# The final norm inside the experts' stage: all rows first, the last three tiles' rows apart

## The chip, the cores and the metric

The kernel runs on one core of a Trainium2 chip. The metric is the device time of one execution in microseconds (us), the median of several. The core has five engines that run on their own and meet at semaphores: TensorE (PE) multiplies matrices, VectorE (DVE) and ScalarE (ACT) work on elements, GpSimd (POOL) issues the indirect DMAs, SyncE (SP) the plain ones. All DMAs run on the core's 16 DMA engines.

## The reference

One decoder layer over 2048 prompt rows and 64 sample rows of 1024 channels. Only its end matters here:

```python
h2 = modulate(rmsnorm(x, prm['norm2_g']), sh2, sc2)
x = x + g2[:, None, :] * hier_moe(h2, ...)      # top-1 of 4 groups, top-2 of its 4 experts
...
y_prompt = rmsnorm(xp, final_norm_g)
y_sample = rmsnorm(xs, final_norm_g)
```

`rmsnorm` divides a row by the root of its mean square plus 1e-6 and multiplies by a gain per channel. Every row goes through exactly two of the 16 experts; an expert is `silu(t @ w_gate) * (t @ w_up)`, times the gate, `@ w_down`.

## The kernel before

`front` and `middle` compute everything up to `h2`. They leave in DRAM `h2_d` (the normed rows), `acc_d` (2112 rows that hold x for the prompt and zeros for the samples, and 128 rows more for the empty places of tiles) and `x2s_d` (x of the samples). `routing` sorts the row numbers by expert into tiles of 128 places. With this input there are 43 tiles, numbered 0 to 42, and `last` is 42.

`experts` takes the tiles in turn. SyncE loads an expert's 3 MiB of weights two experts ahead, once the splits of the expert two before are done (`W.load`). GpSimd gathers a tile's rows from `h2_d` and, four tiles later in its order, scatters a finished tile's rows onto `acc_d` with an adding indirect DMA (`scatter`, line 2241). A scatter waits for the one before it to land, since two tiles can hold the same row, and only then frees its output buffer (`freed`). TensorE transposes the rows, multiplies by gate and up weights, transposes the hidden rows and multiplies by the down weights; each product is made of three, of high and low parts, which ScalarE and VectorE split off. VectorE's `out` (line 2363) multiplies the product by the gating row and leaves it in `o_sb`. ScalarE, VectorE and GpSimd run this in a loop of two tiles a round, with straight code for the last tile. Each engine goes through its own instructions strictly in the order in which they are written; nothing else orders the work.

When all 43 scatters have landed GpSimd raises `all_added`, and `final_norm` begins. SyncE reads `acc_d` in eight pairs of 128-row tiles (1 MiB each, 8 KiB a row) and the sample rows with `x2s_d` (lines 2497 to 2500). For each tile ScalarE squares and sums (2517), VectorE makes the mean (2533), ScalarE the root (2520), VectorE the reciprocal (2535) and the normed rows (2537). SyncE stores each finished pair (2507) and, at the end, waits for all stores.

## Time and profile before

| | us |
|---|---|
| median of 3 executions | 1243.48 (1240.98 to 1244.09) |
| the profiled execution, its own time | 1243.06 |
| its span, first to last instruction | 1241.1 |
| TensorE busy in the span | 1049.5 (85%) |
| VectorE, ScalarE, GpSimd busy | 755.6, 514.4, 258.4 |
| last product on TensorE ends | 1185.2 |
| last scatter lands | 1193.7 |
| last norm on VectorE ends | 1234.9 |

Times in the rows further down are in us from the span's start. A timeline row gives start, duration, engine, source line, operation, what it writes and reads, and in brackets the idle time before it and what ended it. A row of windows gives busy time and count of instructions of each engine in a stretch, then the granted clock of TensorE (1.00 is 2.4 GHz, 0.50 is 1.2 GHz), the mean busy share of the DMA engines and what they moved.

### The profile page before, as it was taken

To read this page: it belongs to the slowest core of one execution; us is meant where nothing else is said; L and a number is where in the kernel's file an instruction comes from. 1 tells how busy PE (TensorE), PEld (TensorE's weight loads), DVE (VectorE), ACT (ScalarE), POOL (GpSimd) and SP (SyncE) were. 2 spreads that over 40 slices of the span, in tenths; PEclk is the share of its full clock that TensorE was granted. 3 is DMA by queue.
4 is the path that set the end of the run, shared out by engine and by line. 5 is a ranking of instruction groups with operands and counts; after the bars stand their busy time and mean duration, and the time that the engine had idled before them with its cause. 6 is when DMAs were issued, how large, how long until landed. Compare 5 with 4: busy or idle time off the path is not lost. (4 is left out here: it accounts for less than half of the span.)

```text
span 1241.1 us, 18046 instructions
## 1 busy us (share of the span) xinstructions
PE 1049.5 (85%) x5428; PEld 798.2 (64%) x5429; DVE 755.6 (61%) x1234; ACT 514.4 (41%) x764; POOL 258.4 (21%) x319
## 2 busy tenths in 40 slices
PE   5599999997568999997999535999999999999910
PEld 3266676674446767786888424887778878778710
DVE  2746475750289983367887686555676555555336
ACT  2522333221152235444665313455655544445325
POOL 0025252534131000000000001233333332232210
PEclk9699999998779999998999857999999999999955
DMA  9814646474592549466766457698789878765479
GB/s 304 324 35 115 205 114 201 118 228 162 147 198 90 167 140 265 157 175 233 239 209 224 134 201 250 163 293 217 218 263 267 223 212 222 220 154 110 88 206 394
DMA packets 173443, 244.74 MB, mean 197 GB/s; under 512 B 70519, under 2 KB 130631, under 8 KB 170263
## 3 DMA queue, kind: packets, MB, share of 16 engines
q1 hardware_dynamic: 148617, 180.31, 45.6%
q0 software_dynamic: 12528, 45.62, 16.1%
q10 hardware_dynamic: 12246, 18.14, 4.2%
q8 instruction: 29, 0.48, 0.1%
q14 instruction: 23, 0.19, 0.0%
HBM read 167.79 MB, written 75.84 MB: 196 GB/s over the span
## 5 line engine op out<-in xcount | busy, mean ns | idle before, releaser
L120 PE MATMUL experts_psGU<-weights_we_hi,experts_x_hi 128*128 (+1 forms) x344 | 144.9, 421 | 8.2 <-DVE experts_x_lo L2344 6.5
L121 PE MATMUL experts_psGU<-weights_we_hi,experts_x_lo 128*128 (+1 forms) x344 | 137.6, 400 | 0.0
L122 PE MATMUL experts_psGU<-weights_we_lo,experts_x_hi 128*128 (+1 forms) x344 | 137.5, 400 | 0.0
L120 PE MATMUL front_psM<-front_hT_hi,front_w_hi 128*128 128x512 f32 x256 | 105.7, 413 | 0.0
L2241 POOL DMA_INDIRECT acc_d<-experts_o_sb,experts_to_col x43 | 72.7, 1690 | 150.3 <-issue 67.0
L121 PE MATMUL front_psM<-front_hT_hi,front_w_lo 128*128 128x512 f32 x256 | 100.4, 392 | 0.0
L122 PE MATMUL front_psM<-front_hT_lo,front_w_hi 128*128 128x512 f32 x256 | 100.1, 391 | 0.0
L120 PEld LDWEIGHTS experts_psGU<-weights_we_hi,experts_x_hi 128*128 128x128 f32 x344 | 65.7, 191 | 34.1 <-issue 19.3
L2344 DVE TENSOR_TENSOR experts_x_lo<-experts_psX,experts_x_hi 128x1024 fp32r<-128x1024 f32 x44 | 53.9, 1225 | 40.1 <-ACT experts_x_hi L2277 40.1
L2334 DVE TENSOR_TENSOR weights_we_lo<-weights_we_raw,weights_we_hi (+1 forms) x64 | 75.5, 1220 | 4.1 <-ACT weights_we_hi L2268 3.1
L122 PEld LDWEIGHTS experts_psGU<-weights_we_lo,experts_x_hi 128*128 128x128 f32 x344 | 65.6, 191 | 15.7
L120 PE MATMUL experts_psD<-weights_wd_hi,experts_hT_hi 128*128 x172 | 72.2, 420 | 1.8 <-DVE experts_hT_lo L2356 1.8
L121 PEld LDWEIGHTS experts_psGU<-weights_we_hi,experts_x_lo 128*128 128x128 f32 x344 | 65.8, 191 | 12.2
L2363 DVE TENSOR_TENSOR experts_o_sb<-experts_psD,experts_g2r 128x1024 f32<-128x1024 f32 x43 | 52.7, 1225 | 26.9 <-PE experts_psD L122 26.9
L2350 DVE SCALAR_TENSOR_TENSOR experts_hid<-experts_sg_e,all_gate,experts_psGU 128x256 f32<-128x256 f32 x43 | 20.7, 480 | 79.4 <-ACT experts_sg_e L2283 79.3
L1991 POOL IOTA routing_io_i<- 128x128 int32 x1 | 0.2, 235 | 329.7 <-POOLq L111 329.7
L122 PE MATMUL experts_psD<-weights_wd_lo,experts_hT_hi 128*128 x172 | 68.6, 399 | 0.0
L121 PE MATMUL experts_psD<-weights_wd_hi,experts_hT_lo 128*128 x172 | 68.4, 398 | 0.0
L2277 ACT CAST experts_x_hi<-experts_psX 128x1024 fp32r<-128x1024 f32 x44 | 44.7, 1016 | 49.1 <-PE experts_psX L2403 49.1
L2268 ACT CAST weights_we_hi<-weights_we_raw (+1 forms) x60 | 59.6, 1043 | 6.6 <-SPq L2221 6.6
L120 PE MATMUL middle_psO<-middle_ws_hi,middle_m_hi 128*128 128x512 f32 (+1 forms) x136 | 56.5, 416 | 5.2 <-DVE middle_m_lo L1743 5.2
L120 PE MATMUL middle_psO<-middle_wp_hi,middle_mp_hi 128*128 128x512 f32 (+1 forms) x136 | 55.0, 404 | 5.8 <-DVE middle_mp_lo L1685 5.8
(441 smaller groups left out, 2442.0 us busy)
## 6 DMA issues: line engine op xcount, KB each, us to landing
front_raw<-in_w_ada SPq DMA_DIRECT2D x32, 512.0 KB, 4.0
weights_we_raw<-in_exp_w_gate SPq DMA_DIRECT2D x16, 1024.0 KB
weights_we_raw<-in_exp_w_up SPq DMA_DIRECT2D x16, 1024.0 KB
weights_wd_raw<-in_exp_w_down SPq DMA_DIRECT2D x16, 1024.0 KB, 13.2
front_raw<-in_w_ada SPq DMA_DIRECT2D x8, 1024.0 KB, 10.9
front_xraw<-in_x_prompt SPq DMA_DIRECT2D x4, 2048.0 KB, 10.0
part_d<-middle_ev ACTq DMA_DIRECT2D x16, 512.0 KB, 3.1
middle_xt<-in_x_prompt SPq DMA_DIRECT2D x16, 512.0 KB, 4.5
```

The source lines that it names most:

```text
L120: pe.matmul(out, l_hi, r_hi, start=start, stop=False)
L121: pe.matmul(out, l_lo, r_hi, start=False, stop=False)
L122: return pe.matmul(out, l_hi, r_lo, start=False, stop=stop)
L1991: pool.iota(io_i[:], [[1, P]], base=0, channel_multiplier=0).then_inc(con, 1)
L2241: pool.indirect_dma_start(acc_d, bass.IndirectOffsetOnAxis(tc[:, u, :], 0), osb[:, u, :], None, compute_op=ALU.add).then_inc(added, 16)
L2268: act.copy(w_hi[:, u, q, :], wraw[:, u, q, :]).then_inc(whi, 1)
L2277: act.copy(x_hi[:, u], psX[:].rearrange("p (k n) -> p k n", k=KD)).then_inc(xhi, 1)
L2334: dve.tensor_tensor(w_lo[:, u, q, :], wraw[:, u, q, :], w_hi[:, u, q, :].bitcast(F32), ALU.subtract).then_inc(wlo, 1)
L2344: dve.tensor_tensor(x_lo[:, u], psX[:].rearrange("p (k n) -> p k n", k=KD), x_hi[:, u].bitcast(F32), ALU.subtract).then_inc(xlo, 1)
L2350: dve.scalar_tensor_tensor(out=hid[:, u, :], in0=sg[:], scalar=R.gate[:, bass.ds(t, 1)], in1=psG[:, u, FH:2 * FH], op0=ALU.mult, op1=ALU.m ...
L2363: dve.tensor_tensor(osb[:, u, :], psD[:], g2r[:, u, :], ALU.mult).then_inc(oev, 1)
```

## The change

`final_norm` is gone as a stage; its work is written at the end of each engine's part of `experts`.

- Tiles 40 to 42 (`end` to `end + 2`) are no longer added to `acc_d` but to a second array, `late_d`, which starts as zeros. `middle` stores a block of zeros (`zero_d`), and SyncE copies it 18 times over `late_d`, two copies of 512 KiB behind each of the weight loads of experts 4 to 12.
- When tile 39's scatter has landed, GpSimd raises `bulk_go`. SyncE then reads six of the eight pairs of `acc_d` into the buffers of the raw weights, which are free by then, and the other two once pairs 0 and 1 are stored. All rows are normed in place and stored into `y_prompt`, whether or not they lack a share of the last three tiles.
- After `all_added` GpSimd gathers the rows of each of the last three tiles from `acc_d`, adds those of `late_d` to them with an adding gather, waits for all plain stores and for the norm of each of these tiles, and scatters them over `y_prompt`. Sample rows and empty places are past the bound and are dropped. The sample rows are summed on VectorE from `acc_d` and `late_d`.
- The loops of ScalarE and VectorE end two tiles earlier; these are written out, without the conversion of a tile 43 that nothing used. On VectorE mean and norm of pair 0 stand ahead of the output of tile 42.

Units 0 to 7 are the pairs, 8 to 10 the late tiles, 11 the samples.

```diff
+                sp.dma_start(zero_d, zero).then_inc(s["gw_in"], 16)
+                sp.wait_ge(s["gw_in"], 48)
...
+LATE = 3
+ROW_PAIRS = TP // P // 2
+UNITS = ROW_PAIRS + LATE + 1
+LATE_BLOCKS = (TOK + 2 * P - 1) // P
...
+        PAIR = 2 * D * 4
+        homes = [("we_raw", 0), ("we_raw", PAIR), ("wd_raw", 0), ("we_raw", 2 * PAIR), ("we_raw", 3 * PAIR), ("wd_raw", PAIR)]
+        rows = [k.over(f"rows{g}", [P, 2, D], homes[g % 6][0], F32, homes[g % 6][1]) for g in range(ROW_PAIRS)]
+        fix = k.over("late_rows", [P, LATE, D], "we_hi")
+        xs = k.over("sample_rows", [TS, D], "we_hi", F32, LATE * D * 4)
+        x2 = k.over("x2", [TS, D], "we_hi", F32, (LATE + 1) * D * 4)
+        xl = k.over("late_samples", [TS, D], "we_hi", F32, (LATE + 2) * D * 4)
+        FREE = {0: (W.wlo, 4 * (NE - 1)), 2: (W.dlo, NE - 1), 3: (W.wlo, 4 * NE), 5: (W.dlo, NE)}
+        SQ = list(itertools.accumulate([2] * ROW_PAIRS + [1] * (LATE + 1)))
...
+        pair = lambda x, g: x.rearrange("(p j) d -> p j d", p=P)[:, 2 * g:2 * g + 2, :]
+        y_p, y_s = o["y_prompt"][0], o["y_sample"].rearrange("b t d -> (b t) d")
...
+        def unit(n):
+            if n < ROW_PAIRS:
+                return [rows[n][:, r, :] for r in range(2)]
+            return [fix[:, n - ROW_PAIRS, :]] if n < UNITS - 1 else [xs[:]]
...
+                for j in range(2 * (e - 2), min(2 * (e - 1), LATE_BLOCKS)):
+                    if j >= 0:
+                        sp.dma_start(late_d[j * P:(j + 1) * P, :], zero_d).then_inc(zeroed, 16)
             sp.wait_ge(F.rows_in, 32)
+            sp.wait_ge(bulk_go, 1)
+            for g in range(6):
+                if g in FREE:
+                    sp.wait_ge(*FREE[g])
+                sp.dma_start(rows[g][:], pair(acc_d[0:TP, :], g)).then_inc(px_in[g], 16)
+            for g in range(ROW_PAIRS):
+                sp.wait_ge(pair_done, g + 1)
+                sp.dma_start(pair(y_p, g), rows[g][:]).then_inc(py_out[g], 16)
+                if 1 <= g < ROW_PAIRS - 5:
+                    sp.wait_ge(py_out[g - 1], 16)
+                    sp.dma_start(rows[g + 5][:], pair(acc_d[0:TP, :], g + 5)).then_inc(px_in[g + 5], 16)
+                if g == 2:
+                    sp.wait_ge(R.all_added, 1)
+                    sp.dma_start(x2[:], x2s_d[:, :]).then_inc(s_in, 16)
+                    sp.dma_start(xs[:], acc_d[TP:TOK, :]).then_inc(s_in, 16)
+                    sp.dma_start(xl[:], late_d[TP:TOK, :]).then_inc(s_in, 16)
+            sp.wait_ge(s_done, 1)
+            sp.dma_start(y_s, xs[:]).then_inc(s_out, 16)
...
-            end = pool.value_load(R.tab[0:1, 1 + 2 * NCOL:], min_val=NE - 2, max_val=MAXT - 2)
-            for d in range(3):
-                scatter(end + d, d % 2)
-            pool.wait_ge(added, end * 16 + 48)
+            end = end_tile(pool)
+            pool.wait_ge(added, end * 16)
+            pool.sem_inc(bulk_go, 1)
+            pool.wait_ge(zeroed, 16 * LATE_BLOCKS)
+            for d in range(LATE):
+                scatter(end + d, d % 2, late_d)
+            pool.tensor_copy(tcf[:], R.to[:, bass.ds(end, LATE)]).then_inc(late_ok, 1)
+            pool.wait_ge(late_ok, 1)
+            pool.wait_ge(added, end * 16 + 16 * LATE)
             pool.sem_inc(R.all_added, 1)
+            for d in range(LATE):
+                pool.indirect_dma_start(fix[:, d, :], None, acc_d, bass.IndirectOffsetOnAxis(tcf[:, d:d + 1], 0)
+                                        ).then_inc(late_in[d], 16)
+            for d in range(LATE):
+                pool.wait_ge(late_in[d], 16)
+                pool.indirect_dma_start(fix[:, d, :], None, late_d, bass.IndirectOffsetOnAxis(tcf[:, d:d + 1], 0),
+                                        compute_op=ALU.add).then_inc(late_in[d], 16)
+            for g in range(ROW_PAIRS):
+                pool.wait_ge(py_out[g], 16)
+            for d in range(LATE):
+                pool.wait_ge(late_done, d + 1)
+                pool.indirect_dma_start(y_p, bass.IndirectOffsetOnAxis(tcf[:, d:d + 1], 0), fix[:, d, :], None,
+                                        bounds_check=TP - 1, oob_is_err=False).then_inc(late_out, 16)
...
+            def squares(n):
+                if n < ROW_PAIRS:
+                    act.wait_ge(px_in[n], 16)
+                elif n < UNITS - 1:
+                    act.wait_ge(late_in[n - ROW_PAIRS], 32)
+                else:
+                    act.wait_ge(s_x3, 1)
+                for r, x in enumerate(unit(n)):
+                    if n or r:
+                        act.wait_ge(sq, SQ[n] - len(unit(n)) + r)
+                    act.activation(junk[0:x.shape[0], :], x, ACT.Square, accum_out=part(n, 0)[:, r:r + 1]).then_inc(sq, 1)
+            def root(n):
+                act.wait_ge(ms, n + 1)
+                act.activation(part(n, 2), part(n, 1), ACT.Sqrt).then_inc(rt, 1)
...
-            with act.Fori(1, last + 1, 2) as t:
+            end = end_tile(act)
+            with act.Fori(1, end + 1, 2) as t:
...
+            hidden_hi(end + 1)
+            silu(end + 2, 0)
+            gate_rows(end + 1, 1)
+            hidden_hi(end + 2)
+            gate_rows(end + 2, 0)
+            squares(0)
+            root(0)
+            squares(1)
+            for n in range(2, UNITS):
+                squares(n)
+                root(n - 1)
+            root(UNITS - 1)
...
+            def mean(n):
+                dve.wait_ge(sq, SQ[n])
+                dve.tensor_scalar(part(n, 1), part(n, 0), 1.0 / D, EPS, ALU.mult, ALU.add).then_inc(ms, 1)
+            def norm(n):
+                dve.wait_ge(rt, n + 1)
+                ch.link(dve.reciprocal(part(n, 3), part(n, 2)))
+                for r, x in enumerate(unit(n)):
+                    ins = dve.scalar_tensor_tensor(out=x, in0=x, scalar=part(n, 3)[:, r:r + 1], in1=F.gn[0:x.shape[0], :],
+                                                   op0=ALU.mult, op1=ALU.mult)
+                ins.then_inc(pair_done if n < ROW_PAIRS else late_done if n < UNITS - 1 else s_done, 1)
+            def sample_sum():
+                dve.wait_ge(s_in, 48)
+                ch.link(dve.tensor_tensor(xs[:], xs[:], xl[:], ALU.add))
+                dve.tensor_tensor(xs[:], xs[:], F.g2[:], ALU.mult).then_inc(gated, 1)
+                dve.wait_ge(gated, 1)
+                dve.tensor_tensor(xs[:], xs[:], x2[:], ALU.add).then_inc(s_x3, 1)
...
-            with dve.Fori(1, last + 1, 2) as t:
+            end = end_tile(dve)
+            with dve.Fori(1, end + 1, 2) as t:
...
+            hidden_lo(end + 1)
+            hidden(end + 2, 0)
+            out(end + 1, 1)
+            hidden_lo(end + 2)
+            mean(0)
+            norm(0)
+            out(end + 2, 0)
+            mean(1)
+            for n in range(2, UNITS):
+                if n == UNITS - 1:
+                    sample_sum()
+                mean(n)
+                norm(n - 1)
+            norm(UNITS - 1)
...
-def final_norm(k, a, o, acc_d, x2s_d, R, F):
...
+        late_d = k.dram("late_d", [LATE_BLOCKS * P, D])
+        zero_d = k.dram("zero_d", [P, D])
...
-                for part in (route, expert, final):
+                for part in (route, expert):
...
```

VectorE at the end of the experts' stage. Before (`hT_lo` and `o_sb` are of tile 42, then the norm of the first 128 rows and the samples' sum):

```order
L2356 TENSOR_TENSOR experts_hT_lo<-experts_psHT,experts_hT_hi 128x256
L2363 TENSOR_TENSOR experts_o_sb<-experts_psD,experts_g2r 128x1024
L2533 TENSOR_SCALAR final_norm_ss_7205<-final_norm_ss_7205 128x1
L2535 RECIPROCAL final_norm_ss_7205<-final_norm_ss_7205 128x1
L2537 SCALAR_TENSOR_TENSOR final_norm_y<-final_norm_x_7201,final_norm_ss_7205,routing_gn 128x1024
```

Now, from the same `hT_lo` on (`rows_7205` and `rows_7206` are pairs 0 and 1):

```order
L2478 TENSOR_TENSOR experts_hT_lo<-experts_psHT,experts_hT_hi 128x256
L2491 TENSOR_SCALAR experts_ss_7203<-experts_ss_7203 128x2
L2495 RECIPROCAL experts_ss_7203<-experts_ss_7203 128x2
L2497 SCALAR_TENSOR_TENSOR experts_rows_7205<-experts_rows_7205,experts_ss_7203,routing_gn 128x1024 x2
L2485 TENSOR_TENSOR experts_o_sb<-experts_psD,experts_g2r 128x1024
L2491 TENSOR_SCALAR experts_ss_7203<-experts_ss_7203 128x2 x2
L2495 RECIPROCAL experts_ss_7203<-experts_ss_7203 128x2
L2497 SCALAR_TENSOR_TENSOR experts_rows_7206<-experts_rows_7206,experts_ss_7203,routing_gn 128x1024 x2
```

The output of the last tile moved behind a whole pair's norm.

VectorE further on, now, from pair 6 (`rows_7211`) to the samples; `rows_7212` is pair 7:

```order
L2497 SCALAR_TENSOR_TENSOR experts_rows_7211<-experts_rows_7211,experts_ss_7203,routing_gn 128x1024 x2
L2491 TENSOR_SCALAR experts_ss_7203<-experts_ss_7203 128x1
L2495 RECIPROCAL experts_ss_7203<-experts_ss_7203 128x2
L2497 SCALAR_TENSOR_TENSOR experts_rows_7212<-experts_rows_7212,experts_ss_7203,routing_gn 128x1024 x2
L2491 TENSOR_SCALAR experts_ss_7203<-experts_ss_7203 128x1
L2495 RECIPROCAL experts_ss_7203<-experts_ss_7203 128x1
L2497 SCALAR_TENSOR_TENSOR experts_late_rows<-experts_late_rows,experts_ss_7203,routing_gn 128x1024
```

The first mean of one column (128x1) is unit 8's, and stands ahead of pair 7's norm.

GpSimd behind its loop. Before, the last scatter and the end:

```order
L2234 COPY experts_to_col<-all_to 128x1
L2236 REGISTER_ALU
L2238 REGISTER_ALU
L2241 DMA acc_d<-experts_o_sb,experts_to_col 2240x1024
L2257 REGISTER_ALU
```

Now, from the last scatter on:

```order
L2300 COPY experts_to_col<-all_to 128x1
L2302 REGISTER_ALU
L2304 REGISTER_ALU
L2307 DMA late_d<-experts_o_sb,experts_to_col 2304x1024
L2326 COPY experts_to_late<-all_to 128x3
L2328 REGISTER_ALU
L2331 DMA experts_late_rows<-acc_d,experts_to_late 128x1024 x3
L2335 DMA experts_late_rows<-late_d,experts_to_late 128x1024 x3
L2341 DMA out_y_prompt<-experts_late_rows,experts_to_late 2048x1024 x3
```

Nine indirect DMAs stand behind the last scatter, three of each kind.

## Rows read from the trace of the kernel before

**Rows 1.** Chain of waits near the end: start, us, what.

```profile
1180.74 6.04 DMA acc_d<-experts_o_sb,experts_to_col
...
1187.63 6.04 DMA acc_d<-experts_o_sb,experts_to_col
...
1193.79 5.50 DMA final_norm_x<-acc_d
...
1200.48 1.28 ACT L2520
```

**Rows 2.** Windows of 10 us in the final stage.

```profile
1190.00:1200.00 10.00, 0.00 (x0) 0.00 (x0) 0.00 (x0) 0.68 (x1) 0.00 (x0) 0.50 0.78 208
1200.00:1210.00 10.00, 0.00 (x0) 0.00 (x0) 7.18 (x13) 5.89 (x14) 0.00 (x0) 0.50 1.01 372
...
1220.00:1230.00 10.00, 0.00 (x0) 0.00 (x0) 8.18 (x18) 6.64 (x17) 0.00 (x0) 0.50 1.01 427
```

**Rows 3.** DMA from 1190 to 1242, and SyncE's last wait (us, times, longest).

```profile
DMA packets 2672, 18.02 MB, mean 347 GB/s; under 512 B 320, under 2 KB 320, under 8 KB 624
...
SPq L2592 <- DMA out_y_prompt<-final_norm_y: 5.4, 1, 5.4
```

**Rows 4.** Timeline of GpSimd: the last gather, the scatters of tiles 39 and 40.

```profile
1157.61 1.00 POOL L1907 DMA_INDIRECT weights_xg<-h_d,weights_idx_col  x1 [0.79 <-POOL weights_idx_col L1904]
...
1161.57 1.59 POOL L2241 DMA_INDIRECT acc_d<-experts_o_sb,experts_to_col  x1 [2.76 <-issue]
...
1171.21 1.58 POOL L2241 DMA_INDIRECT acc_d<-experts_o_sb,experts_to_col  x1 [7.85 <-DVE experts_o_sb L2363]
```

**Rows 5.** Windows around that gather and scatter.

```profile
1161.00:1162.00 1.00, 1.00 (x6) 0.82 (x5) 0.00 (x0) 0.00 (x0) 0.43 (x1) 1.00 0.22 90
...
1164.50:1167.00 2.50, 2.50 (x17) 2.15 (x16) 0.48 (x1) 1.16 (x2) 0.00 (x0) 1.00 0.99 184
1167.00:1173.00 6.00, 6.00 (x28) 4.71 (x27) 2.87 (x3) 1.75 (x3) 1.78 (x2) 1.00 0.00 0
```

**Rows 6.** Timelines: GpSimd's scatters beside a load, SyncE's load, ScalarE's first split of it.

```profile
938.72 1.59 POOL L2241 DMA_INDIRECT acc_d<-experts_o_sb,experts_to_col  x1 [2.75 <-issue]
...
949.57 2.54 POOL L2241 DMA_INDIRECT acc_d<-experts_o_sb,experts_to_col  x1 [4.05 <-DMA acc_d<-experts_o_sb,experts_to_col]
...
919.57 0.37 SPq L1915 DMA_DIRECT2D weights_we_raw<-in_exp_w_gate  x1
...
945.27 2.94 ACT L2268 CAST weights_we_hi<-weights_we_raw  x3
```

**Rows 7.** Windows of one round of two tiles, and its parts.

```profile
919.00:938.00 19.00, 19.00 (x93) 15.16 (x92) 13.04 (x14) 11.14 (x14) 6.76 (x8) 1.00 0.92 270
...
929.00:934.00 5.00, 5.00 (x29) 4.14 (x28) 3.19 (x5) 1.10 (x3) 2.58 (x2) 1.00 1.09 409
934.00:938.00 4.00, 4.00 (x19) 3.08 (x18) 2.77 (x3) 4.00 (x4) 1.20 (x2) 1.00 0.97 237
```

**Rows 8.** Timeline of VectorE: last weight split, outputs of tiles 40 and 42, final norm.

```profile
1132.76 2.32 DVE L2340 TENSOR_TENSOR weights_wd_lo<-weights_wd_raw,weights_wd_hi  x1
...
1169.02 1.23 DVE L2363 TENSOR_TENSOR experts_o_sb<-experts_psD,experts_g2r 128x1024 f32<-128x1024 f32 x1 [0.52 <-PE experts_psD L122]
...
1185.21 1.23 DVE L2363 TENSOR_TENSOR experts_o_sb<-experts_psD,experts_g2r 128x1024 f32<-128x1024 f32 x1 [5.07 <-PE experts_psD L122]
...
1203.41 1.21 DVE L2528 TENSOR_TENSOR final_norm_x<-final_norm_x,routing_g2s 64x1024 f32<-64x1024 f32 x1
...
1206.41 1.28 DVE L2537 SCALAR_TENSOR_TENSOR final_norm_y<-final_norm_x,final_norm_ss,routing_gn 128x1024 f32<-128x1024 f32 x1
```

**Rows 9.** Timeline of ScalarE: its last gating row, then the final stage.

```profile
1179.06 1.24 ACT L2294 ACTIVATE experts_g2r<-experts_g,all_sample,all_prompt 128x1024 f32<-128x1024 f32 x1
1199.32 1.06 ACT L2517 ACTIVATE final_norm_junk<-final_norm_x 128x1024 bf16<-128x1024 f32 x1 [19.02 <-DMA final_norm_x<-acc_d]
1200.28 0.19 ACT L2517 ACTIVATION_READ_ACCUMULATOR final_norm_junk<-final_norm_x 128x1 f32 x1
```

**Rows 10.** Timeline of TensorE after its last wait.

```profile
1180.57 0.49 PE L120 MATMUL experts_psD<-weights_wd_hi,experts_hT_hi 128*128 x1 [1.82 <-DVE experts_hT_lo L2356]
...
1182.91 0.63 PE L120 MATMUL experts_psD<-weights_wd_hi,experts_hT_hi 128*128 x1
1183.33 0.63 PE L121 MATMUL experts_psD<-weights_wd_hi,experts_hT_lo 128*128 x1
```

123 lines of the change are left out of this document (47 added, 76 removed).

## The prediction

> **What bounds the kernel now.** I read the tail of the chain of waits first [rows 1]: after the last expert product it holds two scatters of 6.04 us that follow each other, the first read of accumulated rows (5.50) and the load of the square root's table (1.28). Then the windows [rows 2]: from 1190 to 1200 no engine but DMA works. From 1200 on the 16 DMA engines are full (share 1.01, 372 to 427 GB/s), and the reader should see that VectorE, which the chain names there, is only about as slow as they are. The last 51 us move 18.02 MB [rows 3]. The tail is thus a serial handover of some 20 us, then some 40 us of bytes. The experts' stage before it is TensorE's (busy 20 of 20 us in most windows; it is 19 of 19 in the window of [rows 7]), and none of its products change.
>
> **The early share.** The waits ahead of `bulk_go` end when tile 39's scatter has landed. It is issued at 1161.57 [rows 4] and DMA falls silent at 1167.0 [rows 5], so six pair reads can start at about 1167.2 where the first now starts at 1193.79. They meet a queue that moves nothing for 6 us [rows 5]. One pair is 1 MiB, 2.6 us at 400 GB/s; the first takes 5.5 alone [rows 1]. Six are in by about 1186, unless the scatters take their share. Before, this reading cost the path at least the 5.5 us of the first.
>
> **What the early reads cost the last scatters.** Alone a scatter takes 6.04 us from issue to landing. Beside a weight load it takes about 10.2: issued at 938.72, just before the load, and the next issued at 949.57 on its landing, with 0.85 us of handover [rows 1, 4 and 6]. I take:
> - Tile 40: issued 1171.21 as now, among the reads: 10.3, lands 1181.5.
> - Tile 41: its issue moves from 1180.74 to 1182.4. Reads run out at about 1187, so 7 us between 6.0 and 10.3, nearer the lone row: lands 1189.4.
> - Tile 42: on VectorE the norm of pair 0 now stands ahead of its output product. ScalarE is free at 1180.3 [rows 9], two squares with their sums take 2.4, the table load 1.3, the root 0.2, the reciprocal 0.2 and two norm steps 2.5, so the product that now starts at 1185.21 ends at 1188.3 instead of 1186.4. Its scatter leaves at 1189.4 + 0.85 = 1190.3. The first stores run beside it: 7.5 us. All sums have landed at 1197.8, against 1193.67 now: 4.1 late.
>
> **The added chain.** Behind it GpSimd issues three gathers of the late tiles' rows, then three adding gathers. A gather takes 1.0 us to issue [rows 4] and 3.8 in all: issued 1157.61, DMA quiet within 1161 to 1162 [rows 5]. Beside other traffic, by the scatter's ratio 10.3/6.04, it is 6.5. Three issues end 3.2 after the start, so the first adding gather leaves at +3.8 to +6.5; I take +5.2, since stores fill the queue then. An adding gather isn't in the trace; nearest is the adding scatter, 6.0 to 10.3, and I take 8, between them. The Trainium skill's page "DMA: Bandwidth & Descriptors" (section Anatomy of one DMA) prices a DMA from GpSimd at about 2.0 us plus its bytes at 436 GB/s, which is 3.2 for half a MiB; the scatter's row shows 6.04, so the row decides, and with the page's figure the sum would be 4.8 us shorter. The first late rows are complete at 1197.8 + 5.2 + 8 = 1211.0.
>
> From there the order of work on VectorE and ScalarE counts, priced from [rows 8 and 9]. VectorE's mean of unit 8 (the first late tile; units 0 to 7 are the pairs) stands ahead of pair 7's norm, so pair 7, long in SBUF, waits for the late rows. The bulk pairs 1 to 6 need 2.8 us each from 1188.3 and end near 1205; they are hidden. After 1211.0: square and mean 1.5, pair 7's reciprocal and norm 2.9, the norms of two late units (1.65 each) 3.3, three sample additions and products of 1.22 with their links 3.8, square, root and reciprocal 1.7, the third late norm 1.5: 14.7 us. Then its scatter over `y_prompt`, 3.8 (gather) to 6.0 (adding scatter), 5 with the middle row taken, 0.3 for the handover and 0.5 to the span's end. The sample's store and pair 7's (5.4 for 1 MiB [rows 3]) end within that.
>
> End: 1211.0 + 14.7 + 0.3 + 5 + 0.5 = 1231.5, where the span now ends at 1241.1: 9.6 less.
>
> **The zeroing.** 18 copies of 512 KiB from memory to memory, two behind each of nine weight loads. At 400 GB/s two take 2.6 us; if both the read and the write count, 5.2. The weights themselves have room: a load issued at 919.57 has moved by 934 and its first split starts at 945.27, 11 us later [rows 6 and 7]. Tight are the four successive 19.3 us rounds from 881 to 958, where DMA is busy 0.92 or 0.93 of the time ([rows 7] has one of the four), so 17.8 us; with 2.6 more it is 20.4 and each round runs 1.1 late, 4.4 in all. A scatter may lag 7.4 us before VectorE's next output waits (scatter 39 issued 1161.57, next output 1169.02 [rows 4 and 8]). So the sum of it is hidden; I put 1 us for jitter. In the middle stage one more 512 KiB store stands ahead of the matrix loads, which are not used for another 20 us: nothing. Two fewer conversions of an unused tile, the loops one round shorter and the straight code behind them: between -1 and +1, taken as nothing, since VectorE starts one output 9.6 us after the other there and is busy for a third of that [rows 5 and 8].
>
> **Sum.** 9.6 less, 1.0 more: 8.6 less than the profiled execution's 1243.06 (its span is 1241.1), which is 0.4 under the median of 1243.48. That is 1234.5 beside the execution, and I say 1235.
>
> **Rivals.** (a) The chain at the lone prices. Tile 41 lands 1188.4, 42 leaves 1189.3 and lands 1195.3, gather and add 9.8, scatter 3.8: end 1224.4, time 1226.4 plus 1. For it: VectorE paces the stores at 1 MiB in 2.8 us, so gaps are left. Against: 400 GB/s is about what the queue does at best [rows 2].
> (b) The chain at the loaded prices. 41 lands 1192.7, 42 at 1203.9, +6.5 and +10.3 give 1220.7; with 14.7, 0.3, 6 and 0.5 the span ends at 1242.2, time 1244 and, with the 1 us, 1245: no change. GpSimd's issues can stretch too, as one scatter issue of 2.54 beside VectorE's splits shows [rows 6]. For it: stores, reads and sample rows are about 8 MB between 1190 and 1213, nearly a full queue.
> (c) Slower: the zeroing stalls TensorE. At 5.2 us a round the four rounds take 23.0 of 19.3 us, 14.8 late in all, 7.4 of it through the slack, so 7.4 us of stall. TensorE's granted clock fell from 1.00 (2.4 GHz) towards 0.50 (1.2 GHz) after one idle of 1.82 us, and products came 0.43 apart instead of 0.23 [rows 10], some 1.8 us per such stall; four add 7. Time 1234 + 14 = 1248. It decides from about 4.9 us a pair of copies on. The Trainium skill's page "DMA: Bandwidth & Descriptors" (section Latency and other measured facts) gives 214 GB/s as the full rate of one memory-to-memory copy, 4.9 us a pair; by it the sum would be this rival's. No run of this case shows such a copy of size, and large plain rows may well move faster.
> (d) The change doesn't do what it says: the six reads wait for a weight buffer or for POOL, start near 1194 and all the added chain comes on top: 1243 + 17 = 1260. Against it: the last weight split ends at 1135.1 [rows 8], far ahead.
>
> **Numbers.** My forecast, 1231 to 1240, has 0.5; (a) 0.17; (b) 0.18; (c) 0.13; (d) 0.02. The range 1227 to 1247 leaves out most of (c), (d) and the edge of (a). A measurement of this kernel tells 0.3%, 3.7 us, from no change: faster (under 1239.7) 0.63, within 0.24, slower (over 1247.2) 0.13.
>
> **What would show it.** Right: pair reads at 1167 to 1168; tile 40's scatter at 10 us; VectorE's output of tile 42 after two norm steps; pair 7's norm only behind the first late square; about 33 us from `all_added` to the end; TensorE's idle time in the experts' stage unchanged. Wrong: scatters that take 6 us beside the reads (then 1227), adding gathers of over 10 us, or TensorE waiting on products between 881 and 987.

## The result, and the profile after

The changed kernel takes 1255.82 us (median of 4 runs, 1254.52 to 1258.26) beside 1243.57 (4 runs, 1240.98 to 1244.09): ratio 1.0106, 95% interval 1.0089 to 1.0123. It is slower by 12 us, where 8.6 us less was forecast. The profiled execution took 1258.26 us, the longest of the four; its span is 1256.2. One run below was slow (1527.2 us, the kernel of experiment 7), and its ratio leaves that run out.

The end of its chain of waits (start, us, what), to be laid beside [rows 1]:

```profile
1175.36 10.57 DMA late_d<-experts_o_sb,experts_to_col
1186.78 7.93 DMA late_d<-experts_o_sb,experts_to_col
1195.55 10.75 DMA late_d<-experts_o_sb,experts_to_col
1207.12 1.02 POOL experts_late_rows L2331
1208.45 0.96 POOL experts_late_rows L2331
1209.71 14.62 DMA experts_late_rows<-acc_d,experts_to_late
1224.59 11.99 DMA experts_late_rows<-late_d,experts_to_late
...
1244.49 1.30 DVE experts_late_rows L2497
1246.57 1.42 POOL out_y_prompt L2341
```

Before, two scatters of 6.04 us and one read of 5.50 stood here. Now three scatters of 7.9 to 10.8 stand here, and behind them the third gather (14.62) and the third adding gather (11.99).

Windows of 10 us (the columns of [rows 2]: window, length, busy time of PE, PEld, DVE, ACT and POOL, granted clock, DMA share, GB/s):

```profile
1174.00:1184.00 10.00, 8.96 (x45) 7.12 (x43) 2.58 (x5) 2.89 (x5) 1.77 (x2) 1.00 1.02 370
1184.00:1194.00 10.00, 4.60 (x12) 3.31 (x12) 5.47 (x10) 9.78 (x18) 1.75 (x2) 0.75 1.03 354
...
1214.00:1224.00 10.00, 0.00 (x0) 0.00 (x0) 2.74 (x4) 0.73 (x3) 3.22 (x2) 0.50 1.03 391
1224.00:1234.00 10.00, 0.00 (x0) 0.00 (x0) 2.74 (x4) 1.24 (x3) 1.55 (x1) 0.50 1.03 299
1234.00:1244.00 10.00, 0.00 (x0) 0.00 (x0) 6.64 (x9) 3.46 (x8) 2.29 (x2) 0.50 0.62 220
1244.00:1254.00 10.00, 0.00 (x0) 0.00 (x0) 2.88 (x5) 0.46 (x4) 1.42 (x1) 0.50 0.24 64
```

The DMA engines are full from 1174 to about 1238. From 1214 to 1234 VectorE works 2.74 us in ten, since the late rows have not landed, where it had 8.18 in [rows 2]. In the last two windows the queue is no longer full (0.62, then 0.24), and in the last one every engine mostly waits. The whole stretch moves more than before. DMA from 1165 on, before and after (both windows run to 1275, past the end, so the mean rates are too low; packets and MB can be compared):

```profile
DMA packets 3084, 19.52 MB, mean 177 GB/s; under 512 B 368, under 2 KB 368, under 8 KB 1035
```

```profile
DMA packets 4537, 24.36 MB, mean 221 GB/s; under 512 B 640, under 2 KB 640, under 8 KB 2487
```

SyncE's timeline (start, busy) shows the early share doing what it should, six pair reads at 1172.02, and what followed. The wait for the last sums (6.4 us) held back two pair stores, those of pairs 3 and 4, whose norms had ended at 1201.0 and 1203.7; they left from 1208.17 on, together with the gathers. Pairs 5, 6 and 7 were stored as soon as they were normed:

```profile
1172.02 3.02 SPq L2276 DMA_DIRECT2D experts_rows<-acc_d  x6
...
1206.37 0.48 SPq L2285 DMA_DIRECT2D experts_x<-x2s_d  x1
...
1208.17 1.06 SPq L2279 DMA_DIRECT2D out_y_prompt<-experts_rows  x2
1211.69 0.33 SPq L2279 DMA_DIRECT2D out_y_prompt<-experts_rows  x1
1217.47 0.33 SPq L2279 DMA_DIRECT2D out_y_prompt<-experts_rows  x1
1233.27 0.33 SPq L2279 DMA_DIRECT2D out_y_prompt<-experts_rows  x1
1247.18 0.50 SPq L2289 DMA_DIRECT2D out_y_sample<-experts_sample_rows  x1
```

VectorE's timeline in the same stretch:

```profile
1188.47 2.48 DVE L2497 SCALAR_TENSOR_TENSOR experts_rows<-experts_rows,experts_ss,routing_gn 128x1024 f32<-128x1024 f32 x2
1190.87 1.22 DVE L2485 TENSOR_TENSOR experts_o_sb<-experts_psD,experts_g2r 128x1024 f32<-128x1024 f32 x1
...
1230.47 0.15 DVE L2491 TENSOR_SCALAR experts_ss<-experts_ss 128x1 f32<-128x1 f32 x1 [13.03 <-ACT experts_junk L2392]
...
1230.76 2.48 DVE L2497 SCALAR_TENSOR_TENSOR experts_rows<-experts_rows,experts_ss,routing_gn 128x1024 f32<-128x1024 f32 x2
```

The output of tile 42 stands behind two norm steps, and pair 7's norm behind the first late mean, both as forecast; the 13.03 us of idling ahead of that mean were not. The last surprise is at the very end: DMA falls silent near 1250.2, and the span ends at 1256.2. Waits of SyncE's queue (us, times, longest) at the block's end, after and before:

```profile
SPq L2688 <- PEq L2688: 5.5, 1, 5.5
```

```profile
SPq L2592 <- PEq L2592: 0.2, 1, 0.2
```

One thing must be set aside. Everything from the front stage on lies some 4 us later in this profiled execution: the output product of tile 40 starts at 1173.22 instead of 1169.02 [rows 8]. The kernel of the first experiment has 4.9 us of it in its profiled execution (1173.89 instead of 1169.02) and no difference in its time, and the variants below have from 1.3 (experiment 7, with no zeroing) to 9.8, so this is spread between executions and not a cost. Below it is called the shift; where two traces are compared, it has to be taken out.

### The profile page after: what moved, and what is told of

It is laid out like the page before. It is cut to its first block and busy times, and to the rows that moved or that the text cites. A ratio compares the mean times of both kernels' runs of the same rounds, so it can differ in the third digit from the quotient of the medians.

```text
span 1256.2 us, 18064 instructions
## 1 busy us (share of the span) xinstructions
PE 1050.5 (84%) x5428; PEld 799.7 (64%) x5429; DVE 757.9 (60%) x1227; ACT 515.5 (41%) x764; POOL 274.0 (22%) x329
## 5 line engine op out<-in xcount | busy, mean ns | idle before, releaser
L2307 POOL DMA_INDIRECT acc_d<-experts_o_sb,experts_to_col x40 | 67.8, 1695 | 163.2 <-DMA acc_d<-experts_o_sb,experts_to_col 110.9
## 6 DMA issues: line engine op xcount, KB each, us to landing
weights_wd_raw<-in_exp_w_down SPq DMA_DIRECT2D x16, 1024.0 KB, 13.3
front_raw<-in_w_ada SPq DMA_DIRECT2D x8, 1024.0 KB, 10.9
```

The costliest lines, as they stand in the source:

```text
L2307: pool.indirect_dma_start(dst, bass.IndirectOffsetOnAxis(tc[:, u, :], 0), osb[:, u, :], None, compute_op=ALU.add).then_inc(added, 16)
```

## The experiments

All ratios are to the kernel before, run on the same chip beside each.

### 1. Is it the zeroing?

The kernel before with `zero_d`'s store and the 18 copies; `late_d` is used by nothing.

```diff
+                sp.dma_start(zero_d, zero).then_inc(s["gw_in"], 16)
...
+                for j in range(2 * (e - 2), min(2 * (e - 1), 18)):
+                    if j >= 0:
+                        sp.dma_start(late_d[j * P:(j + 1) * P, :], zero_d).then_inc(zeroed, 16)
```

> The kernel before with the block of zeros stored in the middle stage and the 18 copies of it behind the weight loads; nothing reads them. Theory Z (the zeroing costs what the experts' stage started late, 4 us in the two traces, and more): 1247 to 1248. Theory Q (the tail alone lost the time, the late start is spread between executions): 1243.5 to 1244.5, and TensorE's waits in the experts' stage as before.

Measured: 1243.79 beside 1242.66 us, ratio 1.0003 (0.9986 to 1.002). No cost. The second of the four crowded rounds, first before, then with the copies (windows):

```profile
900.30:919.60 19.30, 19.30 (x94) 15.41 (x93) 13.35 (x14) 11.42 (x13) 6.50 (x9) 1.00 0.92 272
```

```profile
904.30:923.60 19.30, 19.30 (x94) 15.44 (x93) 13.33 (x14) 11.47 (x14) 6.08 (x8) 1.00 1.02 326
```

TensorE stays busy 19.30 of 19.30 us. 54 GB/s more in 19.3 us is the 1 MiB of two copies, and the DMA share rose by 0.10, so a pair costs the 16 engines some 1.9 us, not 5.2. A full queue can hide a part of a price, but from 795 to 1010, where the share was 0.76 to 0.86 before, the same sum gives 1.4 to 1.8 us a pair. Rival (c)'s price was too high.

### 2 and 3. Are the stores in the way of the gathers?

hold_stores lets no store from pair 3 on leave before the adding gathers have landed; samples_last moves SyncE's wait for the last sums, with the samples' loads, from pair 2 to pair 6, so the stores leave before the gathers.

```diff
# hold_stores, behind the samples' loads
+                    for d in range(LATE):
+                        sp.wait_ge(late_in[d], 32)
# samples_last
-                if g == 2:
+                if g == 6:
```

> The changed kernel, but SyncE stores pair 3 and the later ones only when the late rows' adding gathers have landed. Theory Q (the gathers and adding gathers were slow for the stores beside them): a gather lands 3.8 us after its issue and the first adding gather 6 to 7 us after its own, instead of 10.1 and 12.0; the first late square comes some 11 us after the last sum has landed, instead of 23; the time falls to about 1248, since the held 4 MiB then run beside the norms. Theory P (these gathers are that slow by themselves): still 10 and 12 us, and the time rises by the held stores, to 1260 or more.

Measured: 1257.65 us, ratio 1.0119 (1.0089 to 1.0149), against 1.0106 for the changed kernel: nothing gained, and 10 us over what theory Q gave. GpSimd's first gather and first adding gather, its DMA issues by kind (KB each where known, median us to landing), of 1205 to 1260, and a window in which only the adding gathers were under way:

```profile
1208.44 1.02 POOL L2333 DMA_INDIRECT experts_late_rows<-acc_d,experts_to_late  x1 [8.83 <-DMA late_d<-experts_o_sb,experts_to_col]
...
1218.56 1.58 POOL L2337 DMA_INDIRECT experts_late_rows<-late_d,experts_to_late  x1 [5.97 <-DMA experts_late_rows<-acc_d,experts_to_late]
```

```profile
experts_late_rows<-acc_d,experts_to_late POOLq DMA_INDIRECT x3, 9.9
experts_late_rows<-late_d,experts_to_late POOLq DMA_INDIRECT x3, 7.1
out_y_prompt<-experts_late_rows,experts_to_late POOLq DMA_INDIRECT x3, 3.3
```

```profile
1222.00:1228.00 6.00, 0.00 (x0) 0.00 (x0) 1.80 (x4) 1.71 (x4) 1.55 (x2) 0.50 1.03 195
```

For the plain gathers theory Q failed: the first adding gather left 10.1 us after the first gather (1218.56 - 1208.44), exactly as in the changed kernel, though no store from pair 3 on was under way. The queue was full without them (share 1.02 and 315 GB/s over these ten us), with pair 7's read, the samples' loads and the gathers themselves. The adding gathers did land sooner (7.1 instead of 12.0 us), and the first late unit was ready at 1224.98 instead of 1229.29, although this execution lay 1.2 us later. But the held stores then ended near 1244, and the scatters over y_prompt had to wait for them: they left from 1245.17 on. The time was moved, not saved. While three adding gathers ran alone the engines were all busy at 195 GB/s, less than half of the 427 that [rows 2] has.

> The changed kernel, but SyncE waits for the last sum and reads the sample rows behind the store of pair 6 instead of pair 2, so that stores 3 to 6 leave as their norms end (from 1204) instead of at 1208. Theory Q: tile 42's scatter gets slower (10.8 to 12 or so) but the gathers behind it meet some 3 MB less: 1251 to 1254 in all. Theory P: the same 1256 within 1 us.

Measured: 1253.69 us, ratio 1.0095 (1.0064 to 1.0126), as theory Q had it. Against the changed kernel the intervals overlap, so a gain is not shown.

### 4. The gathers ahead of the last scatter

```diff
             for d in range(LATE):
+                if d == 2:
+                    pool.tensor_copy(tcf[:], R.to[:, bass.ds(end, LATE)]).then_inc(late_ok, 1)
+                    pool.wait_ge(late_ok, 1)
+                    pool.wait_ge(gu_mm, end + 2)
+                    for c in range(LATE):
+                        pool.indirect_dma_start(fix[:, c, :], None, acc_d, ...)
                 scatter(end + d, d % 2, late_d)
```

> The changed kernel, but the three gathers from acc_d (whose rows are final once tile 39 has landed) are issued ahead of tile 42's scatter. Theory Q and P both take the 10.1 us between the last sum and the first adding gather off the chain, and give back some for three more transfers ahead of tile 42's scatter: Q expects 5 us back there, since the queue is full of reads and stores (1250 to 1252); P, which lets each indirect transfer cost its own time only, expects 3.5 us back, the issues (1248 to 1250).

Measured: 1251.27 us, ratio 1.0079 (1.0053 to 1.0105), within Q's numbers. By the ratios it is 3.4 us under the changed kernel, and the intervals overlap. GpSimd's timeline (in brackets the idle time before, and what ended it):

```profile
1193.46 1.64 POOL L2307 DMA_INDIRECT late_d<-experts_o_sb,experts_to_col  x1 [2.16 <-DMA late_d<-experts_o_sb,experts_to_col]
1207.53 1.55 POOL L2337 DMA_INDIRECT experts_late_rows<-late_d,experts_to_late  x1 [12.43 <-DMA late_d<-experts_o_sb,experts_to_col]
...
1236.92 1.02 POOL L2343 DMA_INDIRECT out_y_prompt<-experts_late_rows,experts_to_late  x1 [23.25 <-issue]
```

The adding gathers leave at 1207.53 instead of 1217.24, 9.7 us sooner, of which 2.1 are shift. About half of the rest is lost again: the last scatter takes 13.3 us to land, the adding gathers 15.4, and the scatters over y_prompt end a wait of 23.25 us for the pair stores. Some 3 us come out at the end, if any.

### 5 and 6. The two halves of the change, each alone

no_repair leaves out every gather, norm and scatter of the late rows, so their last share is missing from y_prompt; late_reads keeps them all and frees the six early reads only when all sums have landed.

```diff
# no_repair
-UNITS = ROW_PAIRS + LATE + 1
+UNITS = ROW_PAIRS + 1
-            for d in range(LATE):
-                pool.indirect_dma_start(fix[:, d, :], None, acc_d, ...
...
# late_reads
-            pool.sem_inc(bulk_go, 1)
             pool.wait_ge(zeroed, 16 * LATE_BLOCKS)
...
             pool.sem_inc(R.all_added, 1)
+            pool.sem_inc(bulk_go, 1)
...
-            mean(0)
-            norm(0)
             out(end + 2, 0)
+            mean(0)
+            norm(0)
```

> The changed kernel without the repair of the late rows: no gathers, no adding gathers, no norms and no scatters of them, so the last three tiles' share is missing from the rows of y_prompt. Zeroing, early reads, the three scatters to late_d and the samples stay. Theory Q: the repair is the price of the change, as a chain and as bytes. The sums have landed at about 1202 to 1206, pair 7 is read and stored and the samples are stored some 18 us behind that: 1221 to 1226, some 30 us under the changed kernel, and that far under the kernel before by half. Theory R: the bytes after the sums bound it, the repair only adds 4.7 MB of them (12 us at 400 GB/s) and the wait at the end (5.5): 1237 to 1240.

> The changed kernel with its six early reads given free only when all sums have landed, and pair 0's norm behind tile 42's output product (it would wait for ever ahead of it); all of the repair stays. Theory Q: the early share is worth its bytes, 6 MiB that move ahead of the last scatters, 16 us at 400 GB/s, less what those scatters gain when alone (two of them 6.0 instead of 7.9 and 10.7, tile 40's 6 instead of 10.6, and 1.9 for the norm, some 8 in all since one hides the other in part): 1262 to 1266. Theory P: the early share brought nothing, because the scatters ran that much longer: 1253 to 1258, the changed kernel's own time.

Measured: without the repair 1230.92 us, ratio 0.9897 (0.9867 to 0.9927); with the reads late 1270.56 us, ratio 1.0224 (1.0165 to 1.0283); the kernel before, beside both, 1243.64. With the changed kernel this makes a square, in which the kernel before stands for the corner that has neither:

| us | without the repair | with the repair |
|---|---|---|
| reads after the last sums | 1243.6 | 1270.6 |
| reads early | 1230.9 | 1255.8 |

The early share is worth 12.7 us in one column and 14.8 in the other; the repair costs 27.0 in one row and 24.9 in the other. Within the intervals (some 7 us for late_reads, 4 for no_repair) the two are independent, and the repair costs about twice what the early share gives. Both expectations fell short: no_repair lies between Q and R, and late_reads is 5 us over Q. The windows of no_repair, at its end:

```profile
1200.00:1210.00 10.00, 0.00 (x0) 0.00 (x0) 4.64 (x6) 2.39 (x5) 0.00 (x0) 0.50 1.02 354
1210.00:1220.00 10.00, 0.00 (x0) 0.00 (x0) 6.57 (x8) 2.88 (x6) 0.00 (x0) 0.50 1.02 367
1220.00:1222.00 2.00, 0.00 (x0) 0.00 (x0) 1.27 (x3) 0.96 (x4) 0.00 (x0) 0.50 1.00 422
1222.00:1224.00 2.00, 0.00 (x0) 0.00 (x0) 1.97 (x4) 0.00 (x0) 0.00 (x0) 0.50 0.26 111
```

The queue is full up to 1222. Then VectorE's norms of pair 7 and of the samples and the last two stores follow, and the span ends at 1228.9. So even without a repair the early share doesn't give the 26 us by which its reads start earlier (1167.8 instead of 1193.79). The engines are full behind it and move 350 to 370 GB/s where [rows 2] has 372 and 427, and pair 7 is read late (see experiment 11).

The repair's 25 us can be read off the two traces. The reads start 1.7 us later in the changed kernel's (1172.02 and 1170.36). It keeps the queue full to 1238 instead of 1222, so 14 us more. Behind that no_repair needs 6.9 us to its end; the changed kernel has 12 us of chain up to the last scatter's landing at 1250.2, which is 5 more, and then 6 us of nothing. 14 + 5 + 6 = 25.

### 7 and 8. The six us of nothing

To the kernel before is added one plain indirect scatter from GpSimd to a scratch array, behind the last norm (tail_scatter) or behind the twelfth (tail_gap).

```diff
+        def final_pool(pool):
+            pool.wait_ge(y_done, NT)          # tail_gap: NT - 5
+            pool.indirect_dma_start(tail_d, bass.IndirectOffsetOnAxis(R.to[:, 0:1], 0), gn[:], None).then_inc(tail_out, 16)
+            pool.wait_ge(tail_out, 16)
```

> The kernel before, with one plain indirect scatter of 512 KiB from GpSimd added behind the last norm (it writes rows of gn to a scratch array that nobody reads), and waited for. In the changed kernel, whose last work is such a scatter, the span ended some 6 us after DMA had fallen silent. Theory E: a program whose GpSimd has just done an indirect DMA ends about 5.5 us later, whatever it moved. Then the span ends 5.5 us after the scatter lands, and the time is 1243.5 + 1 to 2 for the scatter beside the last store + 5.5 = 1249.5 to 1251. Theory N: the wait at the end belongs to something else of the changed kernel (its 18 zeroing copies, its many queues). Then there is no such wait, and the time is 1244 to 1245.5.

> As tail_scatter (the kernel before with one plain indirect scatter from GpSimd to a scratch array), but the scatter is issued after the twelfth of 17 norms instead of the last, some 9 us earlier, near 1227. Theory H: the 5.5 us at the end run from GpSimd's last DMA on, so they are over before the last store has landed. Then SP's wait at the end is back to about 0.2 us and only the 0.5 MB in the full queue is left, 1.3 us: 1244 to 1245.5. Theory F: whoever has indirect DMAs of GpSimd in this last part of the program pays 5.5 us at its end: 1247.5 to 1250.

Measured: 1247.81 beside 1243.64 us, ratio 1.0039 (1.0024 to 1.0053), and 1243.95 beside 1242.85, ratio 1.0007 (0.999 to 1.0023). The waits of SyncE's queue at the end, tail_scatter first:

```profile
SPq L2599 <- PEq L2599: 5.5, 1, 5.5
```

```profile
SPq L2599 <- PEq L2599: 0.2, 1, 0.2
```

So the wait needs neither the zeroing nor the many queues of the changed kernel. Where an indirect DMA of GpSimd is the last work, SyncE waits at the block's end: tail_scatter's was issued at 1236.17 and landed 4.9 us later, and the span ended at 1245.6, 9.4 us behind the issue (9.6 in the changed kernel). In tail_gap the scatter was issued at 1232.42 and landed 8.4 us later, 5.9 us before the end, and the wait is gone. The wait came as theory E said; the time rose by 4.2 and not by 6, since the last store and that scatter ended side by side. That it runs from GpSimd's last DMA on (theory H) is what the pair shows. The other traces agree: in the ten kernels with such a scatter among their last work, the changed kernel and experiment 12 with them, the span ends 8.1 to 9.7 us behind its issue, however long SyncE waits. In hold_stores, where SyncE's own stores were done early, it waits twice as long:

```profile
SPq L2690 <- PEq L2690: 10.6, 1, 10.6
```

What the chip does in that time, no row says; and whether a plain DMA or any other late instruction of GpSimd would bring it too, no run tried.

### 9. Four edits together

early_gather with the samples' loads behind pair 6's store, pair 7's root and norm ahead of the first late unit, and pair 0's norm behind tile 42's output (the diff below has SyncE's edit and VectorE's norm of pair 7 alone).

```diff
-                if g == 2:
+                if g == 6:
...
+                if n == ROW_PAIRS:
+                    norm(n - 1)
                 mean(n)
-                norm(n - 1)
+                if n != ROW_PAIRS:
+                    norm(n - 1)
```

> The changed kernel with four edits together: the plain gathers of the late rows issued ahead of tile 42's scatter, the samples' loads and their wait behind pair 6's store instead of pair 2's, pair 7's root and norm ahead of the first late unit, and pair 0's norm behind tile 42's output product. Theory Q: the four prices nearly add: early gathers 4.5 less, samples 2.1 less (both measured), two orders of norms 2 to 3 less, and the stores of pairs 3 to 6 are gone before the adding gathers start: 1239 to 1245. Theory R: the queue is full from 1174 on, so what is moved ahead only pushes other bytes back, and the wait at the end stays: 1248 to 1251.

Measured: 1252.53 us, ratio 1.0067 (1.0044 to 1.009). Theory R comes near; early_gather alone was at 1.0079, with intervals that overlap. No gain beyond it is shown. The chain of waits shows one thing that was lost:

```profile
1225.30 12.15 DMA experts_late_samples<-late_d
1237.48 1.23 DVE experts_sample_rows L2508
```

The samples' loads, now issued behind the stores, land 12.15 us later, and the third late norm waited for them.

### 10. Plain gathers instead of adding ones

On early_gather: the rows of `late_d` go into an array of their own, and VectorE adds them.

```diff
-                pool.wait_ge(late_in[d], 16)
-                pool.indirect_dma_start(fix[:, d, :], None, late_d, ..., compute_op=ALU.add)
+                pool.indirect_dma_start(fix2[:, d, :], None, late_d, ...)
...
+                dve.tensor_tensor(fix[:, d, :], fix[:, d, :], fix2[:, d, :], ALU.add).then_inc(lsum, 1)
```

> early_gather with its three adding gathers made plain gathers into rows of their own, which VectorE adds (one step of 1.2 us for each late tile). In hold_stores adding gathers kept the 16 DMA engines full at some 195 GB/s, half of what plain rows move, so each may take the queue 2.7 us instead of 1.3. Theory Q: that doubled queue time counts, 4 us for three, and a plain gather lands sooner (12 instead of 15), less 1.2 us for VectorE's sum: 2 to 4 us under early_gather's 1251.3, so 1247 to 1249.5. Theory R: the final scatters wait for the stores anyway, and these for other bytes; what the adding gathers take is made up elsewhere: 1250.5 to 1252.5.

Measured: 1251.63 us, ratio 1.0062 (1.0042 to 1.0082), not told apart from early_gather. The gathers landed in 10.9 us instead of 15.4, but again the first scatter over y_prompt ended a long wait for the stores, and the last one (1245.01) waited for the third late norm, which stands behind the samples:

```profile
1239.88 1.17 POOL L2344 DMA_INDIRECT out_y_prompt<-experts_late_rows,experts_to_late  x1 [22.82 <-issue]
```

### 11. One late tile

`LATE = 1`: tiles 40 and 41 are added to `acc_d` as before, and the reads are freed behind 41's scatter. The plain gather is issued ahead of tile 42's scatter, and pair 0's norm stands behind tile 42's output (neither is in the diff below).

```diff
-LATE = 3
+LATE = 1
...
+            for d in range(2):
+                scatter(end + d, d % 2)
+            pool.wait_ge(added, end * 16 + 32)
             pool.sem_inc(bulk_go, 1)
...
+            scatter(end + 2, 0, late_d)
```

> The changed kernel with one late tile instead of three (its plain gather issued ahead of tile 42's scatter, pair 0's norm behind tile 42's output product): tiles 40 and 41 are added to acc_d as before, and the reads are given free when 41's scatter has landed. Theory Q: the early share is then worth only the 6 us by which tile 42's scatter and its handover come later, and the repair costs one gather, one adding gather and one scatter over y_prompt, some 2.5 MB of queue or 4 us, 3.6 us for the scatter behind the last store and 5.5 us at the end: 1243.6 - 6 + 4 + 3.6 + 4.5 = 1247 to 1250. Theory R: most of the repair's price is the chain of three gathers and three adding gathers, with one it is cheap: 1240 to 1243.

Measured: 1254.12 us, ratio 1.0085 (1.0055 to 1.0115), slower than both theories, and not told apart from the kernel with three late tiles. It moves 21.59 MB from 1165 on instead of 24.36, but its reads start at 1192.43 instead of 1172.02. (Its profiled execution was its slowest, 1260.55 us.) One link that the sum for it lacked: there are six row buffers for eight pairs, so pair 7 is read only when pair 1's store has landed. In its chain of waits:

```profile
1210.19 11.41 DMA out_y_prompt<-experts_rows
1221.61 13.04 DMA experts_rows<-acc_d
```

Those are 24 us for a store and a read of 1 MiB each in a full queue, and they stand in no_repair's chain too (3.94 and 12.52). The kernel before has room to issue all eight reads in a row.

### 12. The third late norm ahead of the samples

```diff
                 if n == UNITS - 1:
+                    norm(n - 1)
                     sample_sum()
                 mean(n)
-                norm(n - 1)
+                if n < UNITS - 1:
+                    norm(n - 1)
```

> The changed kernel with one order changed on VectorE and ScalarE: the third late tile's root and norm ahead of the samples' sum, square and mean, instead of behind them. In the changed kernel's trace the third late rows were complete at 1236.6 and their norm ended at 1245.8, because the samples' three steps, a square, a mean and a root (5.1 us) stood ahead of it; with them behind, it would end at about 1240.7 and its scatter, behind the second one's issue, leave at 1242.9 instead of 1246.6. Theory Q: the end of the changed kernel is the chain alone (DMA engines are half empty from 1238 on), so what is taken from the chain there is taken from the time: 3.5 us less, 1251.5 to 1253. Theory R: the samples' store then ends last, some 2 us behind today's 1247.2 plus 3.3, and only the 5.5 us at the end overlap with it: 1 to 2 us less, 1253.5 to 1255.

Measured: 1252.91 us, ratio 1.0084 (1.0064 to 1.0104), 2.7 us under the changed kernel by the ratios (0.0022 of 1243), but the intervals overlap. The time lies in Q's range; the 2.7 us lie between Q's 3.5 and R's 1 to 2. The last issues of GpSimd's timeline and of SyncE's, and SyncE's wait at the end:

```profile
1240.64 0.96 POOL L2341 DMA_INDIRECT out_y_prompt<-experts_late_rows,experts_to_late  x1 [0.30 <-issue]
```

```profile
1245.02 0.50 SPq L2289 DMA_DIRECT2D out_y_sample<-experts_sample_rows  x1
```

```profile
SPq L2693 <- PEq L2693: 0.6, 1, 0.6
```

From the first gather's issue to the end it is 1248.8 - 1204.45 = 44.4 us, where the changed kernel has 1256.2 - 1207.12 = 49.1; this compares one of the fastest executions of the one with the slowest of the other. The samples' work and store now lie behind GpSimd's last DMA, and of SyncE's 5.5 us at the end 0.6 are left. The time behind that DMA has not gone: the end is 8.2 us behind its issue (9.6 in the changed kernel), but other work runs in it. The kernel stays slower than before, as every version with a repair did.

## Why the prediction was wrong

**The steps of the sum**, each against the profiled execution, whose shift of 4.2 us is taken out of the second line:

| step | forecast | measured | more |
|---|---|---|---|
| all before tile 40's output | as before | 4.2 late (spread) | 4.2 |
| sums landed | 1197.8 | 1206.35 | 4.35 |
| gathers and first adding gather | 13.2 | 22.9 | 9.7 |
| from there to the third late norm's end | 14.7 | 16.5 | 1.8 |
| handover, last scatter, end | 5.8 | 10.4 | 4.6 |
| end of the span | 1231.5 | 1256.2 | 24.7 |

- **The early share** started as forecast: six reads at 1172.02, which is 1167.8 without the shift. Tile 40's scatter took 10.57 (forecast 10.3), tile 41's 7.93 (7).
- **Tile 42's scatter** took 10.75 where 7.5 was taken, between the lone 6.0 and the loaded 10.3. "The first stores run beside it" was the right observation and the wrong value. The stores of pairs 0 to 2 and the reads of pairs 6 and 7 were issued from 1190.98 to 1199.67, and the queue was full.
- **The gathers** are the step that failed most: the sum's 5.2 + 8 = 13.2 us measured 22.9. The first adding gather left 10.9 us after the last sum (10.1 after the first gather's issue), not 5.2, and it landed 12.05 us later, not 8. The trace of before gave the lone prices rightly: a plain indirect DMA of 512 KiB took 3.3 to 3.6 us to land once the queue was nearly empty (the scatters over y_prompt), an adding gather 7.1 with little beside it. What failed was the load. The prediction bounded "beside other traffic" by one row in which a scatter met one weight load [rows 6]. Here the queue had been full for over 30 us and stayed so. For the adding gathers the stores beside them are shown to be a good part of the load: with these held back, the first took 6.4 us to its landing instead of 12.05 (experiment 2). For the plain gathers they are not: the 10.1 us stayed 10.1 without them, and in the five traces that gather behind the last sum it is 9.1 to 10.1 whatever ran beside. Which of the reads, loads and gathers themselves makes it, and what three gathers take in an empty queue, stays open.
- **The sum also lacked a step**: the DMA engines' own budget. It priced a chain and did not ask whether the bytes fit beside it; only rival (b) counted them, and only up to 1213. They are 23.7 MB from the first early read on. At the mean of the six full windows from 1174 to 1234, 345 GB/s, that is 69 us, so from 1167.8 the queue alone lasts to 1236.5, with the wait at the end still to come; the chain of the sum was over at 1231.5. This fits experiments 2, 4 and 10, which sped up single links by 4 to 8 us and the whole by 0 to 4. It is an argument and not shown: no run changed the bytes alone, and experiment 11, with 2.8 MB less, also started its reads 20 us later.
- **The bulk pairs** were to be normed by 1205. Pair 5's norm ended at 1211.7 and pair 6's at 1217.4, because pairs 6 and 7 are read only into the buffers of pairs 0 and 1, once these are stored, and landed at 1206.5 and 1212.3. The sum had no such link. Here it was hidden behind the gathers.
- **The norms** of the late rows cost 14.7 by the sum and 16.5 in fact, the difference being waits for the second and third adding gather. That pair 7's norm and the samples' steps stand in that chain was right; experiment 12 puts the second of them at 2.7 us, within the noise.
- **The end** was taken as 5 us for the scatter and 0.5 behind it. The scatter took 3.6, and 6.0 came behind. No row of the kernel before could have shown this, since there GpSimd's last scatter had landed 47 us before the end; experiments 7 and 8 show it.
- **The zeroing** was hidden, as forecast (experiment 1), and TensorE's waits in the experts' stage are unchanged within 0.3 us. Rival (c) put a pair of copies at up to 5.2 us of the engines; the measured rise of the share is 1.9. The page "DMA: Bandwidth & Descriptors" of the Trainium skill (section Latency and other measured facts) gives 214 GB/s as the full rate of DMA copies between tensors in memory, by which a pair would take an estimated 4.9 us. This case's trace doesn't bear that out as a price in the shared engines: in a queue that was 0.92 full, the pair added 1.9 us of their time.
- **The rivals.** (b), the chain at the loaded prices, named the right mechanism and ended at 1245, 11 us short. (c) at 1248 and (d) at 1260 lie nearer in number only: TensorE did not stall, and the reads started when they should. (b)'s gather and adding gather (6.5 and 10.3) came out at 10.9 and 12.05, and the 6 us at the end were in none of the cases. The slower side had been given almost wholly to (c), a mechanism in the experts' stage, when the doubtful part was the last 60 us.
- **What would have shown it** named "adding gathers of over 10 us" as a sign of a wrong forecast, and it came. From `all_added` to the end it was 49.9 us and not about 33.

This could have been seen beforehand. The last 51 us before move 18.02 MB [rows 3], and the diff adds three gathers, three adding gathers and three scatters of 512 KiB, which is 4.7 MB (4.8 by the two traces). From 1167.2 on, 22.8 MB at [rows 3]'s own 347 GB/s last to 1233, and the last scatter may leave only behind the last store: with its 5.8 us the end is at 1239, and 2 us are left of the 9.6. The trace, without the shift, ended at 1252.0; this estimate lacks the wait at the end and the lower rate beside adding gathers.

What stays open: how the three terms of the repair (14 us of full queue, 5 of chain, 6 at the end) would shrink if the rows were mended without a second pass over y_prompt. No version here tried that.

## What to carry over

Where the tail of a kernel is bytes, count the bytes of the change first, at the rate that the full windows show, and only then the chain. Reads that started 26 us earlier gave 13 here, since they met a queue that then stayed full. A split that needs a repair pays the repair in the same full queue: measure the two halves apart (here 13 us won, 25 paid) before tuning either, since single links that were sped up by 4 to 8 us gave 0 to 4 at the end. Don't let an indirect DMA of GpSimd be a program's last work: issue it some 10 us before the end and let other work run behind it.

## What the runs showed of the hardware

- With an indirect DMA of GpSimd among the last work, the span ended 8.1 to 9.7 us behind its issue (ten kernels). SyncE's wait at the block's end was what was left of that: 10.6 us in hold_stores, 5.5 in tail_scatter and the changed kernel, 0.6 in late_first, where the samples' norm and store followed; 0.2 in tail_gap, where the scatter left 14 us before the end.
- Three adding gathers kept all 16 DMA engines busy at 195 GB/s (hold_stores); the kernel before has 372 GB/s from 1200 to 1210, where it mostly reads plain rows, and 427 from 1220 to 1230, where it mostly stores them, both at a share of 1.01 [rows 2].
- One indirect DMA of 512 KiB took from 3.3 to 15.4 us to land, by what it did (plain or adding) and what was queued: three plain scatters 3.3 in a queue with nothing else, an adding gather 7.1 with little beside it, 12.0 and 15.4 among pair stores.
- Mixed reads, stores and indirect DMAs held the engines at a share of 0.99 to 1.03 with 299 to 391 GB/s in windows of 10 us of the changed kernel.
- Two copies of 512 KiB from memory to memory beside weight loads raised the share of a 19.3 us round from 0.92 to 1.02, 1.9 us of the engines' time, and TensorE lost none (zero_only).
